# Second block's merge in pairs of output tiles with seven block products, and fewer rotations between the feature pairs

## The reference

```
h = modulate(x, ...);  hc = modulate(ctx, ...)
z = h @ w_in            # retention q/k/v/gate, attention q/k/v/gate, MLP parts, merge logits
o_ret, o_mlp, o_diff = retention(...), chunk_mlp(...), diff_attend(...)   # 512 features each
g_ret, g_mlp, g_diff = split(sigmoid(merge_logits), 3)                    # 1024 features each
y = g_ret * (o_ret @ w_bo[0]) + g_mlp * (o_mlp @ w_bo[1]) + g_diff * (o_diff @ w_bo[2])
out = y @ w_o           # the same for the context in the first layer
```

## Time and profile before

| what | value |
|---|---|
| median of 3 runs | 2534.18 us (2533.37 to 2538.09) |
| profiled execution | 2533.43 us; span of the trace 2531.6 us |
| mean granted TensorE clock | 0.991 |
| busy share of TensorE, VectorE, ScalarE, GpSimd | 97%, 48%, 31%, 20% |

### The profile page before, as it was taken

One profiled execution on the slowest core, in us unless ns is written; L12 is line 12 of the kernel. 1 busy time (PEld: TensorE's weight loads), 2 busy tenths in 40 slices (PEclk: granted clock), 3 DMA queues, 4 the chain that ended last, 5 costly groups with the idle time before them and its releaser, 6 DMA issues.

```text
span 2531.6 us, 63034 instructions
## 1 busy us (share of the span) xinstructions
PE 2456.4 (97%) x27644; PEld 1712.4 (68%) x27644; DVE 1216.1 (48%) x2506; ACT 773.9 (31%) x1552; POOL 493.7 (20%) x502
## 2 busy tenths in 40 slices
PE   6999999999999998999999999999999999999998
PEld 2566666666666666668887887856544468775787
DVE  4766666666666665453652336405511114532412
ACT  3354445545444443131221301024300013102301
POOL 2434333434444341000010043300000000000000
PEclk9999999999999998999999999999999999999999
DMA  7111111111111114544448532220234344431353
GB/s 297 48 39 47 39 46 47 39 38 39 39 48 39 43 40 162 203 149 150 132 134 282 197 107 68 92 78 2 93 131 137 125 140 141 130 120 63 98 156 100
DMA packets 80134, 258.12 MB, mean 102 GB/s; under 512 B 11639, under 2 KB 16984, under 8 KB 79096
## 3 DMA queue, kind: packets, MB, share of 16 engines
q1 hardware_dynamic: 75304, 242.94, 29.7%
q0 software_dynamic: 1360, 5.89, 0.7%
q10 hardware_dynamic: 3200, 5.27, 0.6%
HBM read 253.02 MB, written 1.05 MB: 100 GB/s over the span
## 4 chain that ended last, share of the span: by engine, by line
PE 54%; DVE 3%; DMA 1%; issue 0%; ACT 0%; SPq 0%; DVEq 0%; ACTq 0%
PE ps L2216 10%; PE ps L1952 9%; PE ps L1877 7%; PE ps L2007 6%; PE ps L2233 5%; PE ps L2024 5%; PE ps L2075 4%; PE ps L2120 2%; PE ps L1806 1%; DVE general L2984 1%; PE ps L2140 1%; PE ps L2105 1%; PE ps L2160 1%; PE ps L2099 1%; PE ps L1985 1%; DMA ring<-in_w_mods 1%
## 5 line engine op out<-in xcount | busy, mean ns | idle before, releaser
L2216 PE MATMUL ps<-h,ring 128*128 128x512 f32 (+1 forms) x768 | 256.0, 486 | 0.0
L1952 PE MATMUL ps<-h,ring 128*128 128x256 f32 x1024 | 225.6, 379 | 0.0
L1952 PEld LDWEIGHTS ps<-h,ring 128*128 128x128 f32 x1024 | 193.9, 190 | 34.9 <-issue 9.9
L2216 PEld LDWEIGHTS ps<-h,ring 128*128 128x128 f32 x768 | 145.0, 190 | 101.6 <-issue 91.8
L2007 PE MATMUL ps<-h,ring 128*128 128x256 f32 (+1 forms) x768 | 180.4, 397 | 0.0
L2007 PEld LDWEIGHTS ps<-h,ring 128*128 128x128 f32 x768 | 145.9, 190 | 33.1 <-issue 14.8
L1053 ACT ACTIVATE general<-general 64x512 f32<-64x512 f32 x160 | 101.9, 637 | 163.0 <-DVE general L1252 160.3
L583 PE MATMUL ps<-general,ring 128*128 128x512 f32 x256 | 134.9, 623 | 0.8 <-issue 0.8
L599 PE MATMUL ps<-general,ring 128*128 128x512 f32 x256 | 134.1, 629 | 0.4 <-issue 0.4
L2233 PE MATMUL ps<-general,ring 128*128 128x512 f32 (+1 forms) x384 | 131.0, 486 | 0.0
L774 PEld LDWEIGHTS ps<-general 64*64 64x64 f32 (+1 forms) x5120 | 78.0, 131 | 70.2 <-issue 46.5
(11 more groups left out here) (406 smaller groups left out, 4454.1 us busy)
## 6 DMA issues: line engine op xcount, KB each, us to landing
ring<-in_w_mods SPq DMA_DIRECT2D x88, 512.0 KB, 5.0
ring<-in_w_feature SPq DMA_DIRECT2D x74, 512.0 KB, 3.5
ring<-in_w_rkvg SPq DMA_DIRECT2D x64, 512.0 KB, 3.8
ring<-in_w_in SPq DMA_DIRECT2D x48, 512.0 KB, 3.5
ring<-in_w_merge SPq DMA_DIRECT2D x48, 512.0 KB, 3.5
ring<-in_w_out SPq DMA_DIRECT2D x32, 512.0 KB, 6.2
ring<-in_w_token SPq DMA_DIRECT2D x24, 512.0 KB, 4.0
ring<-in_w_merge SPq DMA_DIRECT2D x48, 256.0 KB, 3.1
```

The costliest lines, as they stand in the source:

```text
L1952: mm = pe.matmul(ps[:, n % 4, 0:NX], weights(key, k), R.h[:, k, 0:NX], start=(k == 0), stop=(k == KD - 1))
L2216: mm = pe.matmul(ps[:, 2 * b, 0:NQ], weights(key, k), R.h[:, k, 0:NQ], start=(k == 0), stop=(k == KD - 1))
```

## The change

Tile 0 and tile 7 of the first layer's merge stay as they are. Tiles 1 to 6 are taken in pairs (1,2), (3,4), (5,6), for each of the three branches: nine groups. A group is two steps of `merge_pair`, the logits (even u, contraction 1024, four matmuls of 256 columns a product) and the branch (odd u, contraction 512, two matmuls a product), each with seven products. GpSimd makes sums of the state and of the three branch inputs (`merge_state_sums`, 16 operations) and of the weight blocks (`merge_weight_sums`, four operations a step). ScalarE copies the first product of each step and takes the sigmoids in two parts. VectorE adds the products up (`merge_adds`) and multiplies (`merge_products`). The loads follow the new order; modulation steps 1 to 5 stand behind groups 0, 1, 2, 4 and 5, the turns behind groups 4 and 7. In the feature pairs a rotation now stands only behind the third and the fifth addition, and the rest of the decay tables comes behind the last pair.

The diff, cut to its core (bank numbers, buffers and the ends of the semaphore chains are left out):

```diff
+ROTATED_AT = (2, 4)
+MERGE_STEPS = {0: 1, 1: 2, 2: 3, 4: 4, 5: 5}
+MERGE_TURNS = {4: 0, 7: 1}
+def merge_group(g):
+    m = 1 + 2 * (g // 3)
+    return m, m + 1, g % 3
+def merge_keys(u):
+    m1, m2, b = merge_group(u // 2)
+    return ("merge", 0, m1, b, u % 2), ("merge", 0, m2, b, u % 2)
...
# TensorE
+    def merge_pair(u):
...
+        K = half // P
+        def product(name, w, side, moving, start=True):
+            for k in range(K):
+                mm = pe.matmul(ps[:, merge_bank(u, name), merge_columns(name)], w[:, side * half + k * P:side * half + (k + 1) * P], moving(k),
+                               start=(start and k == 0), stop=(k == K - 1), skip_group_check=True)
...
+        product("first", one, 0, lambda k: state(k, x)).then_inc(s["m_done"], 1)
...
+        pe.wait_ge(s["m_weight"], 4 * u + 4)
+        product("sixth", sums[1], 0, lambda k: tsum[:, 1, k, :])
+        product("seventh", sums[0], 0, lambda k: tsum[:, 2, k, :]).then_inc(s["m_done"], 1)
...
+        product("fifth", two, 0, lambda k: tsum[:, 0, k, :]).then_inc(s["m_done"], 1)
...
+        product("fourth", two, 1, lambda k: tsum[:, 3, k, :]).then_inc(s["m_done"], 1)
+        pe.wait_ge(s["m_copy"], u + 1)
+        product("first", one, 1, lambda k: state(K + k, x), start=False).then_inc(S.used, 1)
+        pe.wait_ge(s["m_add"], 5 * u + 3)
+        product("fifth", sums[2], 0, lambda k: state(K + k, c), start=False).then_inc(S.used, 1)
...
+        if l == 0:
+            modulation(3, 0)
+            for u in range(2 * MERGE_GROUPS):
+                merge_pair(u)
+                if u % 2 and u // 2 in MERGE_TURNS:
+                    modulation_turn(3, MERGE_TURNS[u // 2])
+                if u % 2 and u // 2 in MERGE_STEPS:
+                    modulation(3, MERGE_STEPS[u // 2])
# ScalarE
+    def merge_group_sigmoids(g):
...
+        merge_copy(u)
...
+        act.activation(sig[:, 0:NX], ps[:, merge_bank(u, "first"), 0:NX], ACT.Sigmoid).then_inc(y["sig"], 1)
+        act.wait_ge(s["m_add"], 5 * u + 5)
+        act.activation(sig[:, NX:], sig[:, NX:], ACT.Sigmoid).then_inc(y["sig"], 1)
+        merge_copy(u + 1)
# VectorE
+    def merge_adds(u, dst):
...
+        dve.tensor_tensor(dst[:, 0, c], region("sixth"), dst[:, 0, x], ALU.add).then_inc(s["m_add"], 1)
...
+        dve.tensor_tensor(dst[:, 1, x], region("seventh"), dst[:, 0, c], ALU.add).then_inc(s["m_add"], 1)
...
+        dve.tensor_tensor(dst[:, 1, c], region("fifth"), dst[:, 1, x], ALU.add).then_inc(s["m_add"], 1)
...
+        dve.tensor_tensor(dst[:, 1, x], dst[:, 1, x], region("fourth"), ALU.subtract).then_inc(s["m_add"], 1)
+        S.through(dve, merge_keys(u)[1])
+        dve.tensor_tensor(dst[:, 0, c], dst[:, 0, c], region("fifth"), ALU.add).then_inc(s["m_add"], 1)
+    def merge_products(g):
...
+        merge_adds(u - 1, W.lsig[g % 2])
+        merge_adds(u, dst)
...
+        dve.tensor_tensor(flat[:, 0:NX], ps[:, merge_bank(u, "first"), 0:NX], sig[:, 0:NX], ALU.mult).then_inc(s["m_first"], 1)
...
+        dve.tensor_tensor(flat[:, NX:], flat[:, NX:], sig[:, NX:], ALU.mult).then_inc(done, 2)
+        if b:
...
+            dve.tensor_tensor(out, out, dst, ALU.add).then_inc(y["prod"], 2)
...
-            later = itertools.chain(turns, part)
             for n in range(PAIRS):
-                for _ in paired(n):
+                for place, _ in enumerate(paired(n)):
                     if n < 2:
                         next(part)
-                    elif n > 4:
-                        next(later, None)
+                    elif n > 4 and place in ROTATED_AT:
+                        next(turns)
# GpSimd
+    def four_sums(dst, src, done, n):
...
+        pool.tensor_tensor(dst[:, 0], low[:, :, c], low[:, :, x], ALU.subtract).then_inc(done, 1)
+        pool.tensor_tensor(dst[:, 2], high[:, :, c], low[:, :, c], ALU.subtract).then_inc(done, 1)
+        pool.wait_ge(done, 4 * n + 1)
+        pool.tensor_tensor(dst[:, 1], high[:, :, c], dst[:, 0], ALU.subtract).then_inc(done, 1)
+        pool.wait_ge(done, 4 * n + 3)
+        pool.tensor_tensor(dst[:, 3], dst[:, 1], high[:, :, x], ALU.subtract).then_inc(done, 1)
+    def merge_state_sums():
+        y = layer[0]
+        pool.wait_ge(y["d_out"], len(diff_jobs(0)))
+        four_sums(W.tsum, R.h, s["m_state"], 0)
+        pool.wait_ge(y["branch"], HEADS)
+        four_sums(W.msum[0], W.F[:, 4 * RG:4 * RG + 4, :], s["m_state"], 1)
+        pool.wait_ge(y["mlp_out"], 4)
+        four_sums(W.msum[1], W.F[:, 4 * MG:4 * MG + 4, :], s["m_state"], 2)
+        pool.wait_ge(y["branch"], 2 * HEADS)
+        four_sums(W.msum[2], W.F[:, 4 * DG:4 * DG + 4, :], s["m_state"], 3)
+    def merge_weight_sums(u):
...
+        S.landed(pool, m1)
+        S.landed(pool, m2)
+        if u >= 4:
+            S.through(pool, merge_keys(u - 4)[1])
+        pool.tensor_tensor(third, one[:, 0:half], two[:, 0:half], ALU.subtract).then_inc(s["m_weight"], 1)
...
     mixing(0)
+    merge_state_sums()
     distances(1)
+    for u in range(2 * MERGE_GROUPS):
+        merge_weight_sums(u)
     mixing(1)
```

More of the change, by code:

```diff
@@ L1601, in pair_keys, with merge_bank, merge_columns @@
     return ("feature", 0, PAIR_FIRST + 2 * n), ("feature", 0, PAIR_FIRST + 2 * n + 1)
+def merge_group(g):
[4 more added lines that the diff above has]
+    return ("merge", 0, m1, b, u % 2), ("merge", 0, m2, b, u % 2)
+def merge_bank(u, name):
+    return (4 * u + {"first": 0, "sixth": 1, "seventh": 1, "fifth": 2, "fourth": 3}[name]) % 6
+def merge_columns(name):
+    return HALF[name == "seventh"]
 def pair_bank(n, name):
@@ L1690, in plan_loads, with merge @@
                 S.add(("token", l, g, q), w_token[g, :, 2 * q:2 * q + 2, :].rearrange("p k n -> p (k n)"))
+        def merge(m, b, x):
+            S.add(("merge", l, m, b, x), w_merge[m, b, :, x * D:x * D + (BW if x else D)], BW if x else D)
         for m in range(KD):
+            if l == 0 and 0 < m < KD - 1:
+                continue
             order = [(0, b) for b in range(3)] + [(1, b) for b in range(3)] if m == 0 else [(x, b) for b in range(3) for x in range(2)]
             for x, b in order:
-                S.add(("merge", l, m, b, x), w_merge[m, b, :, x * D:x * D + (BW if x else D)], BW if x else D)
-            if l == 0 and m < STEPS:
-                modulation(3, m)
+                merge(m, b, x)
+            if l == 0 and m == 0:
+                modulation(3, 0)
+                for u in range(2 * MERGE_GROUPS):
+                    for _, _, tile, b, x in merge_keys(u):
+                        merge(tile, b, x)
+                    if u % 2 and u // 2 in MERGE_STEPS:
+                        modulation(3, MERGE_STEPS[u // 2])
         for side in ((X_HALF,) if l else (C_HALF, X_HALF)):
@@ L1708 @@
     "ctx_loaded", "stored",
-    "t_sum", "w_sum", "p_done", "p_act", "p_dve")
+    "t_sum", "w_sum", "p_done", "p_act", "p_dve",
+    "m_state", "m_weight", "m_done", "m_copy", "m_add", "m_first")
 LAYER_SEMS = (
@@ L2210, in logits @@
         S.landed(pe, key)
-        if m:
+        if m and l == 0:
+            if b == 1:
+                pe.wait_ge(s["m_first"], MERGE_GROUPS)
+            else:
+                pe.wait_ge(s["m_add"], 5 * (2 * MERGE_GROUPS - (1 if b else 2)) + 5)
+        elif m:
             pe.wait_ge(y["sig"], (m - 1) * 3 + b + 1)
@@ L2223, in branch @@
         S.landed(pe, key)
-        if m:
+        if m and l == 0:
+            pe.wait_ge(s["m_add"], 5 * (2 * MERGE_GROUPS - (1 if b else 2)) + (4, 2, 4)[b])
+        elif m:
             pe.wait_ge(y["prod"], (m - 1) * 3 + b + 1)
@@ L2246, in merge @@
             branch(l, 0, b)
[L2247 to L2255, removed]
+        if l == 0:
+            modulation(3, 0)
+            for u in range(2 * MERGE_GROUPS):
+                merge_pair(u)
+                if u % 2 and u // 2 in MERGE_TURNS:
+                    modulation_turn(3, MERGE_TURNS[u // 2])
+                if u % 2 and u // 2 in MERGE_STEPS:
+                    modulation(3, MERGE_STEPS[u // 2])
+        for m in range(1 if l else KD - 1, KD):
+            for b in range(3):
+                logits(l, m, b)
+                branch(l, m, b)
     filt = filters()
@@ L2550, in branches, with merge_copy @@
         roots(HEADS)
+    def merge_copy(u):
+        y = layer[0]
+        g = u // 2
+        x = HALF[X_HALF]
+        m1, _, b = merge_group(g)
+        act.wait_ge(s["m_done"], 4 * u + M_FIRST)
+        if u % 2 == 0:
+            dst = W.lsig[g % 2][:, 0, x]
+            if g >= 2:
+                act.wait_ge(y["prod"], 3 + 2 * (g - 1))
+            else:
+                act.wait_ge(y["branch"], 2 * HEADS)
+        elif b == 0:
+            dst = R.sq[:, m1, x]
+            act.wait_ge(y["branch"], 2 * HEADS)
+        else:
+            dst = W.bout[b - 1][:, 0, x]
+            if g >= 3:
+                act.wait_ge(y["prod"], 3 + 2 * (g - 2))
+            else:
+                act.wait_ge(y["mlp_out"], 4)
```

(43 more changed lines are left out.)

83 lines of the change are left out of this document (71 added, 12 removed).

## The result

| | before | after |
|---|---|---|
| median of 4 runs each | 2533.77 us (2530.94 to 2538.09) | 2512.50 us (2509.46 to 2513.84) |
| profiled execution, span | 2533.43 us, 2531.6 us | 2512.97 us, 2511.2 us |

The ratio is 0.9913, 95% interval 0.9896 to 0.9930: the kernel is faster by 21 us (0.87%). The forecast was 2507.9, range 2497 to 2518; the time lies 4.6 us above the one and inside the other. By the two spans 20.4 us went, where the sum had 25.5, so 5.1 us are to be found.

A forecast was written before the change was run, and what follows sets the result against it. TensorE, busy for 97% of the span, was taken to bound the kernel. From 2533.4 us, -14.9 (rotations), -22.2 (products), +10.6 (merge start) and +1.0 (borders) gave 2507.9 us, range 2497 to 2518.

The forecast's parts named there:

- the sum: Whole kernel: 2533.4 - 14.9 - 22.2 + 10.6 + 1.0 = 2507.9 us, a gain of 25.5.
- Part 1: Feature pairs: with two rotation steps a pair, TensorE's waits and the half clock go, -14.9 us (bounds -7.5 and -14.9).
- half rotations: Rival, feature pairs: rotations still delay them, half of the pairs' saving stays, 2515 us; chance 0.10.
- Part 2: Merge tiles 1 to 6: seven products a step cut TensorE's matmul time from 185.4 to 163.2, -22.2 us.
- bare loads: Rival, merge products: 324 more weight loads overlap no matmul and cost 69 us, 2577 us; chance 0.01.
- Part 3: Merge start: GpSimd's sums hold VectorE, spatial waits 7.0 us, first weight sums come late; +10.6 us (bounds 0 and 15.6).
- the smaller sum by that rule: Merge start: were VectorE's first operation issued ahead of GpSimd's, the fourth would end a sum earlier, 2.3 us lower.
- no collision: Rival, merge start: normed slips in ahead or between and GpSimd's chain stays short, 2497 us; chance 0.18.
- Part 4: Pace of merge groups: all hidden but five borders with a modulation step, 0.2 us each, +1.0 (bounds 0 and 7).
- my bound of 7: Five merge borders: upper bound in us, with all four sums at 1.59 and the landing half a microsecond later.
- The sign that I had named for being wrong: Merge: TensorE waits on m_weight beyond 1 us at the borders (also named: normed at 0.5 us, m_add every step).
- slower: Rival, merge borders: sums late at all five; 5.1 us each undoes the gain, 2540 us at 4 us waiting; chance 0.04.

The follow-up runs named there:

- e4: The changed kernel with the sixth product waiting for three of four weight sums, the fourth awaited later, before the first product's second half: 2503.91 us, ratio 0.9881.
- e3: The changed kernel with GpSimd's state sums of the merge started only after VectorE's four normed operations: 2514.93 us, ratio 0.9920.
- e2: The changed kernel with the old places of the rotations, so only the merge is new: 2527.75 us, ratio 0.9972 to the kernel before.
- e6: The changed kernel with VectorE's two group-end operations cut from 768 and 1024 columns to 8 and 2 x 8: 2507.08 us, ratio 0.9900.

## Why the prediction came out as it did

- **Part 1, right in size and in mechanism.** 157.12 us for 13 pairs against 157.2. The step at a pair's start is held for as long as foreseen and then lets the additions through. VectorE's timeline of after in the pair that starts at 1478.68 + 7 x 12.09 = 1563.3:

```profile
1563.94 5.45 DVE L3136 TENSOR_TENSOR general<-general 32x256 f32<-32x256 f32 x4
1569.42 0.42 DVE L3138 TENSOR_TENSOR general<-general 128x256 f32<-128x256 f32 x1
1569.95 0.42 DVE L3141 TENSOR_TENSOR general<-general 128x256 f32<-128x256 f32 x1
...
1571.34 0.42 DVE L3049 TENSOR_TENSOR general<-ps,general 128x256 f32<-128x256 f32 x1
```

  The third addition ends 8.5 us into the pair (8.3 foreseen), TensorE needs it at 10.4. The rival "half rotations" is out.
- **Part 2, right.** 22.2 us, seen bare where the sums are in time (e4). The 324 extra weight loads cost nothing that this stretch shows, so "bare loads" is out too.
- **Part 3, right in mechanism, a little too large.** 9.3 us against 10.6: 8.5, and 0.74 for the wait for the first weight sums with what stands behind it (from the first group's first record to the start of its product `fifth` 1831.16 - 1825.14 = 6.02 us in after, 1830.15 - 1824.87 = 5.28 in e4). `normed` took the four turns that I gave it:

```profile
1780.14 2.34 POOL L3482 TENSOR_TENSOR general<-h 128x1024 f32<-128x1024 f32 x1 [134.76 <-ACT general L2612]
...
1780.52 9.73 DVE L3217 TENSOR_SCALAR general<-general 128x512 f32<-128x512 f32 x4 [6.04 <-ACT general L2646]
```

  (GpSimd's first sum and the four operations, after.) TensorE waited 6.6 us for them, 7.0 foreseen. `spatial` then took 5.52 us, where it took 3.73 before: 1.8 us for the clock in place of 2.6. The granted clock over its first five microseconds (third number from the end) was 0.65, so part of it ran at the lower level:

```profile
1790.50:1795.50 5.00, 5.00 (x30) 5.00 (x31) 4.86 (x9) 0.00 (x0) 0.00 (x0) 0.65 0.01 3
```

  The Trainium skill, "SBUF — State Buffer" (Who interferes with whom), gives the pair of ports to the instruction that came first, for its whole length; the trace agrees (9.73 us for four operations beside four sums of some 2.4). VectorE's came 0.4 us behind, as I had it, so the smaller sum by that rule did not arise. The rival "no collision" is out.
- **Part 4 is the term that was mis-sized.** I gave the five borders 0.2 us each, 1.0 in all, from a landing of 3.5 us and from "one or two" sums delayed by 0.33. They cost 8.76 - 0.74 = 8.0, above my bound of 7 (the same nine groups, with the start, waited 7.2 us here, 6.8 in e3 and 5.7 in e2, so this price is not the same in every run). The sign that I had named for being wrong came: waits of 2.05, 1.50 and 1.68 us at three of the borders. It is the mechanism of the rival "slower", which I gave 0.04, at a third of the 25.5 us that it needed. Two numbers were wrong. The landing was the median over all loads of the tile, while the load in question is the second of two that follow each other, and took 4.4 in the mean. And I had costed what GpSimd does to VectorE's 768 and 1024 columns and noted that TensorE needs nothing of them soon; what they do to GpSimd, whose sums TensorE does need, I took from rows of 512 columns or less: 0.33, where it was 0.6 and 0.85. With these two operations short (e6), 6.4 of the 8.0 went.
- The books close: borders +7.0, start -1.3 and a start of the pairs that is 0.6 earlier make +5.1, the 5.1 that the forecast was short.

## What to carry to other kernels

When one engine is given work for another's sake, cost the collision in both directions: a long operation that nobody waits for can hold up a short one that the bound engine needs. Where a load has only a few microseconds of slack, take its landing from loads at that place in the queue, not from the median of its kind. And before moving or shrinking work to mend a late operand, see which product reads it first: waiting for three sums in place of four, with no operation changed, gave back 8 us.

## What the runs showed of the hardware

- VectorE's operations out of SBUF lengthen GpSimd's by more the longer they are: a sum of 512 columns took 1.27 us alone, 1.86 beside 768 columns of VectorE's and 2.12 beside 1024, and 1.27 again when these were cut to 8 and 16.
- A short wait of TensorE costs more than its length: six waits of 0.5 to 2.05 us, 7.22 in all, cost 8.76 against the run that has none of them, about 0.26 each on top, with a granted clock of 1.00 behind each of the six.
- Removing a hold of 9.8 us freed only 5.0 of the chain behind it, in a trace where VectorE and GpSimd went on to hold each other in the next stretch (sums of 512 columns at 1.7 us in place of 1.27), and behind the new wait of 2.48 us the granted clock was 0.67 (5.38 us for records that take 3.62).
